# Splitting the output projection's quarters in the prompt attention phase of a hybrid encoder step

## The reference, cut to what matters

```python
q_block 128 rows; 4 heads, each with two 64-wide score maps, values 128 wide
p = softmax(mask(q @ k.T / 8))                  # two maps per head
a = p[:, :, 0] - lam * p[:, :, 1]
o = rms_normalize(a @ v) * subln_w * (1 - lambda_init)
mix = concatenate([ret_out, diff_out], -1) @ w_out      # 1024 x 1024
x = x + rmsnorm(mix, norm_mix_post)
u = rmsnorm(x, norm_ffn_pre) @ w_up
x = x + rmsnorm(square(relu(u)) @ w_down, norm_ffn_post)
```

## Time and profile before

| | |
|---|---|
| median of 3 runs | 3156.98 us (3156.43 to 3160.06) |
| the profiled execution | 3157.81 us, its span 3156.0 us |
| mean granted TensorE clock | 0.964 |
| busy in the span: PE, DVE, ACT, POOL | 2898.0, 1515.4, 926.9, 318.4 us |
| the attention phase | about 900 to 1550 us of the span |

### The profile page before, as it was taken

The page is one execution under the profiler, slowest core; times in us unless marked ns, Lnnn a source line. Parts: engine busy times, 40 slices in busy tenths (PEclk is TensorE's granted clock), DMA queues, the critical chain, the costliest instruction groups (busy, mean ns, idle before and its releaser), DMA issues.

```text
span 3156.0 us, 39293 instructions
## 1 busy us (share of the span) xinstructions
PE 2898.0 (92%) x14977; PEld 2398.6 (76%) x14977; DVE 1515.4 (48%) x2983; ACT 926.9 (29%) x1838; POOL 318.4 (10%) x437
## 2 busy tenths in 40 slices
PE   5999995999968999999589999999968999999997
PEld 4888884778856766766468888888857998998995
DVE  3232333323246777777344444444456445445446
ACT  3222222222125555555331211211142211211212
POOL 0111110111112111111100000000013000000003
PEclk8999997999979999999789999999988999999999
DMA  4111003333332111110221111111124111111112
GB/s 147 32 34 34 34 21 116 111 113 123 117 122 75 64 64 47 52 41 21 107 68 46 54 40 53 40 53 53 40 69 136 51 40 41 53 40 40 53 54 97
DMA packets 105661, 204.64 MB, mean 65 GB/s; under 512 B 11024, under 2 KB 47888, under 8 KB 105552
## 3 DMA queue, kind: packets, MB, share of 16 engines
q1 hardware_dynamic: 103248, 194.79, 18.7%
q0 software_dynamic: 2304, 8.39, 0.8%
HBM read 168.28 MB, written 34.87 MB: 64 GB/s over the span
## 4 chain that ended last, share of the span: by engine, by line
PE 46%; DVE 2%; ACT 1%; DMA 1%; POOL 0%; issue 0%; SPq 0%; POOLq 0%
PE bank L1907 23%; PE bank L1923 22%; DVE ffn_facc L1806 1%; PE bank L120 1%; DVE ffnp_x L113 0%; ACT ffn_hTh L130 0%; DMA ffnp_x<-x_scratch 0%; DVE ffn_facc L1844 0%; POOL ffnp_rstd L108 0%; ACT ffn_relu L96 0%; ACT ffn_relu L1729 0%; DVE ffn_hidl L1829 0%; DMA ffn_raw<-in_w_up_dram 0%; DVE ffn_dnl L1800 0%; DVE ffn_upl L1793 0%
## 5 line engine op out<-in xcount | busy, mean ns | idle before, releaser
L1907 PE MATMUL bank<-ffn_hTh,ffn_uph 128*128 128x352 f32 (+1 forms) x1280 | 452.5, 354 | 23.3 <-DVE ffn_upl L1793 14.2
L1844 DVE TENSOR_TENSOR ffn_facc<-bank,ffn_facc 128x512 f32<-128x512 f32 x510 | 345.1, 689 | 233.4 <-PE bank L1923 233.0
L1907 PE MATMUL bank<-ffn_hTl,ffn_uph 128*128 128x352 f32 (+1 forms) x1280 | 451.5, 353 | 0.0
L1907 PE MATMUL bank<-ffn_hTh,ffn_upl 128*128 128x352 f32 (+1 forms) x1280 | 450.9, 352 | 0.0
L1923 PE MATMUL bank<-ffn_dnh,ffn_hidh 128*128 128x512 f32 x1088 | 427.3, 393 | 6.4 <-DVE ffn_dnl L1800 3.5
L1923 PE MATMUL bank<-ffn_dnh,ffn_hidl 128*128 128x512 f32 x1088 | 425.6, 391 | 0.0
L1923 PE MATMUL bank<-ffn_dnl,ffn_hidh 128*128 128x512 f32 x1088 | 425.5, 391 | 0.0
L1823 DVE SCALAR_TENSOR_TENSOR ffn_relu<-bank,ffn_relu 128x352 f32<-128x352 f32 (+1 forms) x160 | 94.5, 591 | 499.6 <-ACT ffn_relu L1744 499.6
L1907 PEld LDWEIGHTS bank<-ffn_hTh,ffn_uph 128*128 128x128 f32 x1280 | 242.6, 190 | 48.4 <-DVE ffn_upl L1793 14.5
L1907 PEld LDWEIGHTS bank<-ffn_hTl,ffn_uph 128*128 128x128 f32 x1280 | 242.7, 190 | 23.4
L1907 PEld LDWEIGHTS bank<-ffn_hTh,ffn_upl 128*128 128x128 f32 x1280 | 242.7, 190 | 22.7
(11 more groups left out here) (196 smaller groups left out, 4462.3 us busy)
## 6 DMA issues: line engine op xcount, KB each, us to landing
ffn_raw<-in_w_up_dram SPq DMA_DIRECT2D x64, 512.0 KB, 4.4
ffn_raw<-in_w_down_dram SPq DMA_DIRECT2D x64, 512.0 KB, 4.1
ffnp_x<-x_scratch SPq DMA_DIRECT2D x24, 512.0 KB, 4.4
retp_x<-in_x_prompt_dram SPq DMA_DIRECT2D x16, 512.0 KB, 3.6
retw_raw<-in_w_in_dram SPq DMA_DIRECT2D x8, 1024.0 KB, 5.2
dpp_x<-in_x_prompt_dram SPq DMA_DIRECT2D x16, 512.0 KB, 5.1
dp_kst<-in_cache_diff_k_dram SPq DMA_DIRECT2D x32, 256.0 KB, 2.9
mix_xr<-in_x_prompt_dram SPq DMA_DIRECT2D x16, 512.0 KB, 3.3
```

What stands on the lines that cost most here:

```text
L1844: nc.vector.tensor_tensor(out=part, in0=Dn[i % s.rd][:], in1=part, op=ALU.add).then_inc(s_add, 1)
L1907: last = nc.tensor.matmul(U[i % s.ru][:, 0:w], l[:, k, f * P:(f + 1) * P], r[:, k, c:c + w], start=(k == 0 and q == 0), stop=(k == 7 and q ...
```

## The change

Each quarter is cut into two runs of six products (two pieces of the contraction each). The first run stays behind the first two groups of transposes; the second stands at the end of the step, behind the weighing and the last score chunks, and in h0 ahead of the transposes of keys and queries. `mixT(t)` moves from behind the quarter to the end of h1, behind the second run. The planner numbers mixT's pair after all score chunks of the step. On ACT `mT_hi(t)` moves behind all `AT_out` of the step, on DVE `mT_lo(t)` behind all copies and `negmax`. The signal for `y_out` is given by the run that ends a half (pieces 6 and 7). The six quarters behind the loop stay whole.

```diff
@@ plan_pairs
-                if h == 1:
-                    m_pair[t] = next(u)
                 if n + 2 < ntot:
                     for i in range(early(n + 2), len(chunks(items[n + 2][0]))):
                         sc_pair[n + 2, i] = next(u)
+                if h == 1:
+                    m_pair[t] = next(u)
@@ ACT
+                    AT_out(n, slice(2, None))
                     if h == 1:
                         mT_hi(t)
-                    AT_out(n, slice(2, None))
                     if n:
                         meansq_o(n - 1)
@@ DVE
-                    copies(n + 2, slice(0, 2))
+                    copies(n + 2, slice(None))
+                    negmax(n + 2)
                     if h == 1:
                         mT_lo(t)
-                    copies(n + 2, slice(2, None))
-                    negmax(n + 2)
@@ PE
-                def quarter(j, q):
+                def quarter(j, q, part=None):
 
                     b, k0 = q // 2, 4 * (q % 2)
+                    ks = range(k0, k0 + 4) if part is None else range(k0 + 2 * part, k0 + 2 * part + 2)
...
-                    if q == 0:
+                    if q == 0 and not part:
...
-                    if k0 == 0 and (j or b):
+                    if ks[0] == 0 and (j or b):
                         pe.wait_ge(s_y, 2 * j + b)
-                    for k in range(k0, k0 + 4):
+                    for k in ks:
...
-                    if k0:
+                    if ks[-1] == 7:
                         last.then_inc(s_yp, 1)
@@ PE, the loop
                     if quarter_of(n):
-                        quarter(*quarter_of(n))
-                    if h == 1:
-                        mixT(t)
+                        quarter(*quarter_of(n), 0)
                     for g in range(ng):
                         AT_in(n, g + 2)
                         scores(n + 2, 2 + g, 3 + g)
                         weigh(n, g)
                     scores(n + 2, 2 + ng, None)
+                    if quarter_of(n):
+                        quarter(*quarter_of(n), 1)
+                    if h == 1:
+                        mixT(t)
                     if h == 0 and t + 1 < nt:
                         kq(t + 1)
```

## The result

The changed kernel takes 3170.08 us (median of 7 runs, 3168.03 to 3172.75), the kernel before, beside it on the same chip, 3161.11 (7 runs, 3156.43 to 3165.62). The ratio is 1.0029, with an interval of 1.0018 to 1.0041: **slower by 9.0 us**, 5.7 to 13.0. Against the three runs known at the prediction (3156.98) it would be 13; with more runs the kernel before stands 4 us higher. The profiled execution of the changed kernel took 3168.03 us (span 3166.3), 10.2 over the one before. Forecast were 3172, in a range of 3162 to 3181.

What follows compares the result with a forecast made beforehand. PE was taken to bound the kernel; losses of 24.3, less 11.4 and 0.5, plus 1.5 and 0.75 gave +14.7 us on a median of 3157.0, forecast as 3172. Range 3165 to 3178 (chance 0.70), widened to 3162 to 3181 for judging.

Steps and rivals of the forecast that it cites:

- The bound: Stretch from 900 to 1550 us: PE sets the pace, and its 72 us idle is what an edit can change.
- The split's gain: h3 of blocks 7 to 14: score chunks issued 1.42 us earlier shrink the wait to about 0.9; gain 11.4 us.
- The new wait at h2: h2 of blocks 7 to 14: chain of 4.59 us from mixT, covered only 2.79; 1.80 a block, 14.4 in all.
- Block 15: h2's wait 3.72 us against 0.80 before, a loss of 2.9; h3's gain between 0 and 1.42, taken as 0.5.
- y_out: At the end of h3: ACT's later copies stay covered, except at the phase's end, where emptying the bank costs 0.75 us.
- The pairs of score banks: h2 and h3: chunk 2 needs chunk 0's pair sooner; blocks 12 to 14 wait 0.1 to 0.5 us, 1.5 in all.
- PE's work is the same: Six products behind each of 63 of 64 steps: PE's work unchanged, score chunks issued 1.42 us earlier.
- The clock: Granted clock 1.00 around h3's wait of 2.31 us, 0.91 with 0.23 idle: such waits alone do not lower it.
- 1 (faster, the chain covered): h2: DVE's early finish covers the chain, L1451's tile ready by 2.79 us after mixT; 3147 us, chance 0.05.
- 2 (no difference, half the wait): h2 waits half as long, 0.8 to 0.9 us in nine blocks; 3158 us, chance 0.09.
- 3 (the clock swings more): Two waits a block make the clock dip, 1.8 us in each of 15 blocks, costing 27; 3199 us, chance 0.06.
- 4 (ACT late): ACT's copies also late, PE's third transposes wait 1 us a block in blocks 7 to 14; 3180 us, chance 0.10.

Runs made afterwards that it cites:

- Experiment 1: The kernel before with the quarters of h0, h2 and h3 split 6 + 6, h1's whole and mixT unmoved: 3148.37 us against 3160.95, ratio 0.9955.
- experiment 2: Also mixT_end_whole: the changed kernel with whole quarters in front, mixT, mT_hi and mT_lo still at the end of h1; 3186.86 us against 3160.95 before, ratio 1.0082.
- experiment 3: Also h2_split_only: the kernel before with only h2's quarter split 6 + 6, all others whole; 3144.04 us against 3160.95, ratio 0.9940.
- experiments 9 and 11: The kernel before with y_norm queued behind h3's combine on DVE, 3114.64 us; the same with h2's quarter also split 6 + 6, 3113.50 us.

## Why the prediction was right, and where its sum was off

**The bound: right.** PE sets the pace, and the time followed its waits. No instruction was added or removed.

**The split's gain, 11.4 forecast for h3 of blocks 7 to 14: right.** The wait fell by 1.39 (2.31 to 0.92), eight times, 11.1. Experiment 1 has 11.9 less wait and 12.6 less time.

**The new wait at h2, 1.80 a block: right in mechanism, 0.1 too small in all.** The chain is 4.59. Under it PE's own work takes 0.97 for mixT and 1.92 for the two chunks, 2.89, not 2.79: from mixT to the next start it is 0.97 now (1296.98 to 1297.95), where the earlier trace rows have 0.87. L1451 so starts 1.70 late, of which 1.37 shows as idle time. Then its eight transposes take 1.05 instead of 0.85, since the second four follow the second piece of the combine. From L1451 of h1 to the first product of h2 it is 13.71 now (1288.91 to 1302.62). In the kernel before:

```profile
1284.58 1.09 PE L1451 MATMUL bank<-kept_ident,mix_S 128*128 128x128 f32 x8
...
1296.36 0.48 PE L1438 MATMUL bank<-mixw_whi,mix_mTh 128*128 128x512 f32 x1
```

That is 11.78, so **1.93 lost** with the same work; experiment 2 has 13.70, so next to nothing of it is h1's split. In blocks 8 to 14 it is 1.91 to 1.93, in block 7 1.79, in block 6 1.57: 16.8 us, where 16.1 was forecast. Blocks 3 to 6 grew by 0.96, 1.18, 1.36 and 1.61 us in the start of h3's L1451 against the kernel before; forecast were 0.24 x (4, 5 and 6), so 0.96, 1.20 and 1.44, and 1.7.

**Block 15: one term over, one under.** h2's wait is 3.55, where 3.72 was forecast. h3's fell from 4.12 to 2.73, by 1.4: I took 0.5 between bounds of 0 and 1.42, and the upper bound was right. In experiment 1, too, h3's wait there is 2.73, and L1452 of h3 follows that of h2 by 11.25 us, against 12.62 before. PE in block 15:

```profile
1508.19 1.40 PE L1451 MATMUL bank<-kept_ident,mix_S 128*128 128x128 f32 x8 [3.55 <-DVE mix_S L1313]
...
1521.03 1.29 PE L1451 MATMUL bank<-kept_ident,mix_S 128*128 128x128 f32 x8 [2.73 <-DVE mix_S L1313]
...
1530.28 0.50 PE L1438 MATMUL bank<-mixw_whi,mix_mTh 128*128 128x512 f32 x1 [0.75 <-ACT mix_y L1232]
...
1550.32 0.50 PE L1438 MATMUL bank<-mixw_whi,mix_mTh 128*128 128x512 f32 x1 [0.75 <-ACT mix_y L1232]
```

**y_out: right.** The 0.75 is there at 1530.28. The last row answers to 1540.80 of the earlier trace rows: the phase ends 9.5 us later.

**The pairs of score banks, 1.5 us: too large.** PE's waits of that stretch have one of 0.3 us on L1286 and no more. PEld waits 5.2 us for L1286 in 24 places, against 0.7 in 4, but most of it lies under PE's products.

**What the sum left out: the price of a split.** "PE's work is the same" holds nearly: 0.01 in h1 and 0.02 to 0.08 elsewhere (experiment 3), so some 0.1 us a block.

**The terms as measured:** 16.8 (blocks 6 to 14) + 5.3 (blocks 0 to 5, as forecast; of them only 3 to 5 are measured, 3.5 against 3.6) + 2.75 (block 15) - 11.1 - 1.4 + 0.75 + about 1 for the splits + 0.3 = 14.4. The sum forecast was 14.7, but the phase is only 10.9 us longer in the profiled executions (647.5 against 636.7). Most of the 3.5 between is the kernel before's: it loses 1.6 us each to two stretches at half the granted clock, in blocks 10 and 14, and the changed kernel has none in blocks 5 to 14. The first is to be seen in its lag: at h3's L1451 the changed kernel is 5.90 us late in block 10 and 4.91 in block 11 (1308.57 before, 1313.48 now), where the lag grows by 0.5 to 0.7 in blocks 7, 8, 9, 10, 12 and 13. In blocks 0 to 2 both kernels have such stretches, and the lag goes from -1.50 to +0.56 and back to -1.50; there no term can be read.

**The clock: misread.** Against a swing of the clock the prediction set that the window from 1460 to 1480 us has a granted clock of 0.91 with only 0.23 of idle, and concluded that waits like h3's do not bring it down. But the window opens where h3's wait of block 14 ends:

```profile
1460.19 1.42 PE L1451 MATMUL bank<-kept_ident,mix_S 128*128 128x128 f32 x8 [2.44 <-DVE mix_S L1313]
```

From 1460.19 to 1466.00 the granted clock is 0.71, and the 12 products of the quarter take 4.41 us instead of 2.84. So the lower clock followed a wait of this size, and the last section shows that this was no single case.

**Luck in the number.** The measured 3170.08 lies 2 us from the 3172 forecast, but the difference was off by 6: 9.0 against 14.7. The kernel before stands 4 us higher than the three runs known at the prediction had it, which made up for most.

**The rivals.** 1 (faster, the chain covered) is out: it needed a tile by 2.79 after mixT, and it came at 4.59. 2 (no difference, half the wait) is out as a mechanism, since the loss is 1.93 and not 0.9; the time all the same lies between its figure and the forecast. 3 (the clock swings more) is out for the change: it spends 44 us of the phase at half the granted clock, the kernel before 46, and none from 1140 to 1440 us. If anything the split spared a little. 4 (ACT late) is out: PEld's waits for AT_out are 6.5 us in 12, as before, and PE's 0.9.

## What to carry to other kernels

When a producer in the middle of a chain over several engines is moved, count the work of the pacing engine between the chain's start and its consumer, before and after: the chain stayed at 4.59 us, and what changed was the cover. A change that shortens one wait and makes another is worth what the first wait happens to be: +9 us here, +28 once the wait in h3 had gone for another reason. So look first at what makes the late engine late: four lines moved on DVE gave 47 us, where every placing of PE's products together gave 22 at best. The best kernels of this study are those of experiments 9 and 11, at 3114.64 and 3113.50 us, the same within their noise.

## What the runs showed of the hardware

**POOL's addition held one small instruction of DVE.** While L1161 adds two 128x1024 tensors in 2.34 us, DVE's 128x1 L1309 takes 2.39 instead of 0.22; with y_norm moved, the same addition (2.41 us) lies beside copies out of the banks, which keep their 0.61 from one to the next and 0.69 each. L1309 has two SBUF inputs (and a scalar), a copy reads a bank. I had read these rows before the prediction and taken the 2.39 as given, where it was the largest sum to be won. The Trainium skill, "GPSIMD Engine Reference", section "Specifications", says that POOL shares its SBUF interfaces with VectorE, and that the contention is with VectorE's instructions in a 2-port mode or with two SBUF inputs. The trace agrees. How long the hold lasts that section doesn't say; here L1309 ends within 0.02 us of the addition in all 15 blocks, so it lasts for the rest of POOL's instruction. In all 15, too, L1309 stands close behind y_norm, and no run parts the two; that both end together speaks for the addition. An instruction with one input in a bank was not held: behind the loop of the kernel before, L1337 takes its 1.28 for two beside an addition, as elsewhere.

```profile
1531.37 1.28 DVE L1337 TENSOR_TENSOR mix_mTl<-bank,mix_mTh 128x512 fp32r<-128x512 f32 x2
1531.60 2.36 POOL L1161 TENSOR_TENSOR mix_xr<-mix_xr,mix_y 128x1024 f32<-128x1024 f32 x1 [1.46 <-DVE mix_y L1346]
```

**The clock.** Windows from 1140 to 1440 us (length, busy PE, PEld, DVE, ACT, POOL, then granted clock, DMA share, GB/s), of the kernel before, the changed one, mixT_end_whole and h2_split_only in this order:

```profile
1140.00:1440.00 300.00, 284.09 (x1718) 205.65 (x1718) 229.90 (x714) 171.71 (x332) 37.74 (x91) 0.99 0.14 47
```

```profile
1140.00:1440.00 300.00, 284.39 (x1705) 199.15 (x1705) 229.24 (x709) 166.03 (x328) 40.05 (x92) 1.00 0.14 47
```

```profile
1140.00:1440.00 300.00, 274.90 (x1595) 196.16 (x1595) 216.18 (x669) 159.70 (x313) 38.80 (x88) 0.97 0.14 46
```

```profile
1140.00:1440.00 300.00, 292.87 (x1778) 209.97 (x1774) 238.11 (x739) 178.84 (x347) 39.05 (x94) 1.00 0.14 47
```

The kernel with both waits, 1.37 in h2 and 2.3 in h3 of each block, has 0.97, the one before, with h3's alone, 0.99, and those with shorter waits 1.00. The granted clock of a trace is always 1.00 or 0.50. In h3 of blocks 7 to 14 the waits of 2.31 to 2.44 number 16 in two traces, 8 in the kernel before and 8 in mixT_end_whole. Behind 8 of them, 2 and 6, the clock fell to 0.50 between 0 and 1.2 us after PE went on. In the other ten traces h3's waits there are 1.67 or less, and behind none of the 80 did it fall. What one costs is seen in the quarter that follows: 4.42 and 4.41 us for 12 products in blocks 10 and 14 of the kernel before, against 2.84, so 1.6. This also explains why experiments 1 and 2 do not add up to the change: such stretches are 0 and 6 in these two, 2 in the kernel before and none in the change, which leaves 4 x 1.6 = 6.4 us too much in the sum, and in the profiled executions the phase has 7 too much (-11.0 + 28.9 against 10.9). It is one profile of each kernel; the mean granted clock of all timed runs agrees, 0.960 to 0.962 for mixT_end_whole and 0.962 to 0.964 for the change. That the length of the wait decides is argued from these counts and not shown: no run was made for it. The Trainium skill, "TensorE: Matmul & The Clock Gate", section "A second HAM failure mode: psum-queue depth-cycling", describes such an effect of short idles; mixT_end_whole would fit it, the change itself, at 1.00, does not.

**Idle time shown is less than time lost.** In h2 the trace shows 0.52 + 0.85 = 1.37 idle, where start to start 4.59 - 2.89 = 1.70 are lost up to the start of L1451, because the modelled ends of the matmuls cover the rest, and 1.93 up to the next product, because the eight transposes behind the wait take 1.05 instead of 0.85.
